# Ten weight blocks and the first chunk's output in transfers of 120 and 8 partitions

## The reference

```python
def one_chunk(xc):                       # 128 tokens
    q = (xc @ w_q).reshape(PEER_CHUNK, PEER_HEADS, 2, PEER_HALF)
    sc = jnp.einsum('chid,hikd->chik', q, sub_keys)
    top_s, top_i = lax.top_k(sc, PEER_TOPK)
    ...
    expert = i1 * PEER_KEYS + i2
    gate = jax.nn.softmax(best_s, axis=-1)
    u_e = jnp.take(u_tab, expert, axis=0)
    v_e = jnp.take(v_tab, expert, axis=0)
    act = jax.nn.gelu(jnp.einsum('chkd,cd->chk', u_e, xc))
    return jnp.einsum('chk,chkd->cd', gate * act, v_e)

for l in range(DEPTH):
    h = rmsnorm(x, norm_mix_g[l])
    proj = h @ w_in[l]
    ...
    x = x + y @ w_out[l]
    x = x + memory_cross_attention(rmsnorm(x, norm_mem_g[l]), rmsnorm(mem, mem_norm_g[l]),
                                   w_mq[l], w_mkv[l], w_mo[l])
    x = x + peer_ffn(rmsnorm(x, norm_ffn_g[l]), peer_wq[l], peer_sub_keys[l], peer_u[l], peer_v[l])
return rmsnorm(x, final_norm_g)
```

## Time and profile before

| | |
|---|---|
| median of 3 runs | 1695.9 us (1695.7 to 1696.14) |
| the profiled execution's span | 1694.8 us |
| median less span | 1.1 us |
| PE busy | 1540.1 us (91%) |
| DVE busy | 1176.0 us (69%) |
| ACT busy | 734.3 us (43%) |
| POOL busy | 578.1 us (34%) |
| moved by DMA | 675.13 MB, mean 398 GB/s |
| of it by the gathers' queue | 536.90 MB |
| of it by SP's queue | 136.74 MB |

### The profile page before, as it was taken

How to read it: one execution, slowest core, us unless ns; L and a number is a source line. 1 busy time by engine, 2 the same in 40 slices (tenths; PEclk the granted TensorE clock), 3 DMA queues, 4 the chain that set the end, 5 groups by cost and what they waited for, 6 DMA issues and landing times.

```text
span 1694.8 us, 19255 instructions
## 1 busy us (share of the span) xinstructions
PE 1540.1 (91%) x6354; PEld 893.8 (53%) x6354; DVE 1176.0 (69%) x2993; ACT 734.3 (43%) x1963; POOL 578.1 (34%) x527
## 2 busy tenths in 40 slices
PE   9999999889999999988989889988999998777786
PEld 8757775347567656434645446434756554222232
DVE  7821899975877658987555667995556676666655
ACT  4142534763464333484433353465444334333333
POOL 0000444442334334443333433342333444343331
PEclk9999999999999999999999999999999999999999
DMA  9655999999999999999999999999999999999996
GB/s 384 257 199 223 376 422 421 421 421 420 420 420 421 420 419 421 413 422 422 420 421 421 416 421 421 392 417 391 421 413 413 421 421 422 422 421 421 421 421 276
DMA packets 94003, 675.13 MB, mean 398 GB/s; under 512 B 10424, under 2 KB 10704, under 8 KB 12496
## 3 DMA queue, kind: packets, MB, share of 16 engines
q0 software_dynamic: 73728, 536.90, 76.5%
q1 hardware_dynamic: 20032, 136.74, 19.9%
q10 hardware_dynamic: 144, 0.26, 0.0%
HBM read 672.81 MB, written 1.05 MB: 398 GB/s over the span
## 4 chain that ended last, share of the span: by engine, by line
PE 35%; DMA 35%; DVE 9%; ACT 4%; issue 2%; POOL 0%; DVEq 0%; ACTq 0%; POOLq 0%
DMA slots<-expert_rows,expert 35%; PE bank L1007 19%; PE bank L477 7%; DVE slots L2027 5%; PE bank L680 3%; PE bank L974 2%; PE bank L990 2%; ACT diag L1518 1%; ACT coef L1536 1%; DVE sg L1563 1%; DVE htok L1850 1%; PE bank L767 1%; ACT gel L1531 0%; DVE x L1563 0%; ACT L1531 0%
## 5 line engine op out<-in xcount | busy, mean ns | idle before, releaser
L1007 PE MATMUL bank<-slots,diag 128*128 128x512 f32 x1914 | 902.6, 607 | 129.3 <-ACT diag L1518 123.0
L1142 POOL DMA_INDIRECT slots<-expert_rows,expert x512 | 576.2, 1125 | 1092.7 <-PE bank L1007 876.7
L2027 DVE CUSTOM_DVE_ANT_0 slots<-slots,htok 128x1024 f32<-128x1024 f32 x512 | 625.7, 1223 | 389.5 <-DMA slots<-expert_rows,expert 388.5
L1007 PEld LDWEIGHTS bank<-slots,diag 128*128 128x128 f32 x1914 | 346.3, 192 | 546.3 <-issue 324.3
L1531 ACT ACTIVATE gel<-dot 128x2 f32<-128x2 f32 (+1 forms) x258 | 52.5, 203 | 652.2 <-DVE dot L2027 651.5
L477 PEld LDWEIGHTS bank<-hT,ring 128*128 128x128 f32 x1488 | 180.1, 192 | 42.1 <-issue 40.6
L477 PE MATMUL bank<-hT,ring 128*128 128x128 f32 x1488 | 181.2, 276 | 1.5 <-ACT hT L1178 1.0
L1518 ACT ACTIVATE diag<-ident,coef 128x128 f32<-128x128 f32 x479 | 168.2, 394 | 8.6
L1536 ACT ACTIVATE coef<-gel,gexp 128x1 f32<-128x1 f32 x512 | 123.1, 287 | 10.4
L1531 ACT ACT_TABLE_LOAD x67 | 86.0, 1283 | 1.2
L1563 DVE SCALAR_TENSOR_TENSOR sg<-pad,prm,sg 128x128 f32<-128x128 f32 x240 | 71.5, 342 | 0.0
(11 more groups left out here) (359 smaller groups left out, 1475.2 us busy)
## 6 DMA issues: line engine op xcount, KB each, us to landing
ring<-w_blocks SPq DMA_DIRECT2D x89, 1024.0 KB, 9.3
slots<-w_blocks SPq DMA_DIRECT2D x24, 1024.0 KB, 11.1
slots<-expert_rows,expert POOLq DMA_INDIRECT x512, 16.0
kept<-w_blocks SPq DMA_DIRECT2D x4, 1024.0 KB, 12.6
keys<-w_blocks SPq DMA_DIRECT2D x2, 1024.0 KB, 10.4
kv<-w_blocks SPq DMA_DIRECT2D x2, 1024.0 KB, 14.0
prm<-small SPq DMA_DIRECT2D x2, 768.0 KB, 12.7
x<-x_rows SPq DMA_DIRECT2D x2, 512.0 KB, 11.4
```

The lines of the kernel that those rows point to most:

```text
L1007: last = mm(bank[h][:, :], diag[:, i % DIAGS, :], slots[:, SLOT[n], D + h * 512:D + (h + 1) * 512], start=m == 0, stop=n == end - (ph == N ...
L1142: nc.gpsimd.indirect_dma_start(slots[:, s, :], None, (experts0_d, experts1_d)[n // PER // NC], bass.IndirectOffsetOnAxis(ap=idx[q % 2][:, ...
L2027: v.tensor_tensor_reduce(out=slots[:, s, 0:D], in0=slots[:, s, 0:D], in1=htok[:, ph % 2, :], scale=1.0, scalar=0.0, op0=ALU.mult, op1=ALU.add,
```

## The change

`PARTED` names, for stage 1, 2 and 3, three, three and four blocks: `out` 18, `mq` 23 and `mo` 27 in stages 1 and 3, `wq` 31 in stage 3 as well, and `q` 4, `mv` 14 and `mo` 25 in stage 2. Each goes in two transfers, partitions 0 to 119 (`MOST` = 120) and 120 to 127. Both add 16 to `loaded` of the place, so PE waits for the sum of parts (`in_by`). The two stores of the first chunk are split in the same way; `stored` then counts six transfers, four of chunk 0 and two of chunk 1.

```diff
+PARTED = {1: (18, 23, 27), 2: (4, 14, 25), 3: (18, 23, 27, 31)}
+MOST = 120
...
+        def parts(j):
+
+            l, n = order[j]
+            return 2 if n in PARTED.get(NC * l + second[j], ()) else 1
+
+        def in_by(j):
+
+            p, n = spots[j]
+            return 16 * sum(parts(i) for i in range(j + 1) if spots[i][0] == p)
...
-                    eng.wait_ge(loaded[p], 16 * (spots[j][1] + 1))
+                    eng.wait_ge(loaded[p], in_by(j))
...
-                nc.sync.dma_start(home(p), blocks_d[l * NBLK + n, :, :]).then_inc(loaded[p], 16)
+                if parts(j) == 2:
+                    nc.sync.dma_start(home(p)[0:MOST, :], blocks_d[l * NBLK + n, 0:MOST, :]).then_inc(loaded[p], 16)
+                    nc.sync.dma_start(home(p)[MOST:P, :], blocks_d[l * NBLK + n, MOST:P, :]).then_inc(loaded[p], 16)
+                else:
+                    nc.sync.dma_start(home(p), blocks_d[l * NBLK + n, :, :]).then_inc(loaded[p], 16)
...
-                    nc.sync.dma_start(out_d[c * P:(c + 1) * P, i * 512:(i + 1) * 512],
-                                      outs[c][:, i * 512:(i + 1) * 512]).then_inc(stored, 16)
-            eng.wait_ge(stored, 16 * 2 * NC)
+                    for a, b in ((0, MOST), (MOST, P)) if c == 0 else ((0, P),):
+                        nc.sync.dma_start(out_d[c * P + a:c * P + b, i * 512:(i + 1) * 512],
+                                          outs[c][a:b, i * 512:(i + 1) * 512]).then_inc(stored, 16)
+            eng.wait_ge(stored, 16 * (4 + 2))
```

## The result

The changed kernel takes 1744.1 us in the median of four runs (1743.8 to 1745.7), against 1696.0 us before: a ratio of 1.0284, 95% interval 1.0271 to 1.0296. It is 48 us slower, 44 us over my forecast and 30 us over the end of my range. The mechanism was among the rivals, but its price was not.

A forecast was written before the change was run, and what follows sets the result against it. The DMA engines, through the one that ends last, were taken to bound the kernel. Span 1694.8 + 3.5 (blocks) + 0.2 (output) = 1698.5 us; with 1.1 us from span to median, 1699.6 us. Range 1689 to 1714 us.

The forecast's parts named there:

- The bound and the straggler: DMA engines set the pace; the slowest ends some 5.0 us behind the second, with a 9.2 us tail after it.
- Which engine it is: The engine that ends last was taken as one of the eight that get one row more per changed block.
- term (1): Ten split blocks: each gives the last engine one more row plus a packet and completion, 0.35 us; 3.5 us in all.
- The shares of engines: 120 rows go to 15 engines, 8 each, and 8 rows to 8 engines, one each; one engine may get none.
- SP's issues and PE's waits for 32: SP's 12 further issues, 4 us in all, and PE's waits for 32 increments on split blocks cost nothing.
- a sign against this term: PE waiting for `ring` more than a few us in total would show the free SP issues wrong.
- The output: First chunk's output, two transfers become four: two more 2 KB rows and two more completions, 0.2 us.
- the price of a row off the whole block's pattern: Off-pattern 8 KB rows in changed blocks were priced after the `gains` transfers, which cost only 0.04 and 0.08 us.
- The upper bound: Most the changed blocks could cost: each row meets another engine's in SBUF and takes twice as long, 28 us.
- The rival: Rows of split blocks, dealt off their engines' own partitions, collide beside gathers: 14 us more, 1713.6 us; chance 0.24.
- half of nine rows: The collision rival's sizing: half of the nine rows in each changed block take twice as long, 14 us.
- the forecast case: One more row per changed block for the last engine, without collisions: 1698.5 to 1701 us; chance 0.42.

The follow-up runs named there:

- The spread rows: Kernel before plus 28 HBM-to-HBM transfers of eight, seven or fifteen 8 KB rows, every second row of a larger array: 1704.85, 1704.88 and 1705.33 us, against 1696.81.
- fifteen and eight singly: Kernel before, but of the ten blocks only the 120-partition transfers are issued, or only the 8-partition ones: 1731.92 us and 1684.49 us.
- the column halves: Kernel before with the ten blocks each in two transfers of 128 partitions by half the columns, output whole: 1696.95 us, ratio 1.0004.
- the fifteen spread rows: Kernel before plus 28 HBM-to-HBM transfers of fifteen 8 KB rows each, every second row of a larger array: 1705.33 us, ratio 1.0051.

## Why the prediction was wrong

**The bound and the straggler: right.** DMA sets the pace, one engine ends last, alone for some 5 us, and 9.2 us follow its last landing; all of that stands unchanged in the trace after.

**Which engine it is: right.** I took it to be one of the eight from 0.04 and 0.08 us in the earlier trace rows, thin evidence, so there was luck in it. The spread rows confirm it, if transfers to HBM and to SBUF use the same engines. With their 0.29 us a row (forecast: 0.35 with its packet and completion), term (1) comes to 2.9 us where I had 3.5. In the changed kernel itself no run isolates that term.

**The shares of engines: right.** 84 completions more, and fifteen and eight singly.

**SP's issues and PE's waits for 32: right.** Nothing, by the column halves. PE's waits for `ring`, 5.0 us, were more than the few us that I had named as a sign against this term. They follow from the collisions, not from the issues: the column halves have the same issues and wait 1.1 us, and in PE's longest wait the DMA engines stay busy at a low rate:

```profile
401.90:405.30 3.40, 0.01 (x1) 0.04 (x1) 0.00 (x0) 0.00 (x0) 0.94 (x1) 0.87 0.98 265
```

**The output: 0.2 us forecast, about 1 us measured.** That is a difference of two medians whose ranges meet, and no more than a hint. It is the same kind of transfer, with rows of 2 KB.

**The step that failed: the price of a row off the whole block's pattern.** The prediction said: "No row shows off-pattern transfers of 8 KB; the nearest, the `gains` ones, cost only 0.04 and 0.08 us, and I follow them." That row was near in kind and far in size. A `gains` transfer is eight packets under 2 KB on eight engines, one each; the part of 120 partitions alone is 120 rows of 8 KB, and the block is in flight for some ten microseconds. Its cost was not that of an extra row on one engine but of everything that was in flight beside it.

**The upper bound was wrong too,** and this is the more instructive step. "Every row of a changed block meets another engine's row at the same place in SBUF and takes twice as long. That is nine rows of 0.310 us more in ten blocks, 28 us." When two rows meet, both are slow, and the other one is often a gather's. While a changed block lands, an engine moves its eight or nine rows of the block and at least as many of gathers: in ten microseconds at 0.55 us a row, 18 rows. Each takes 0.24 us more than 0.31: 4.3 us a block, 43 us in ten. With the extra row of 2.9 us and the output's 1.1 us that is an estimate of 47 us, against the 48 measured. The queues' shares give the same size without it: 29 us in gathers' rows and 18 us in SP's. The numbers for it stood in my own text: rows of both queues at 0.310 us, a block that lands 9.3 us after its issue, engines without any idle time. Counting whatever is in flight for those 9.3 us, about thirty rows an engine at the old pace, would have given a bound above the result. The range did not even hold the bound that I had: 28 us over the median is 1724 us, and the range ended at 1714.

**The rival was the right one, mis-sized.** "Rows off their engines' own partitions collide" had 24% and 1713.6 us. Its mechanism is the one that the trace shows, down to the sign it named, a rate well under 420 GB/s at a full DMA share. Its "half of nine rows" should have been nearly all rows of both queues. And the forecast case is not another case beside it: by the shares the straggler had its extra row while the collisions happened. I had put as alternatives what could add up.

**What the mechanism rests on.** Shown: column halves cost nothing (1.0004), partition halves with the same engines and shares 39 us, and a split block with no gathers beside it already moves at 0.58 us a row. Not shown: which engine read which row and wrote to which partition, since no view has it; so that the rows meet in SBUF, and not in HBM, is argued, with the fifteen spread rows for it. The Trainium skill, page "DMA: Bandwidth & Descriptors", section "The descriptor swizzle", says that in a transfer of 128 partitions each engine writes to the eight partitions of one SBUF port, its own; transfers of other counts are not covered by that formula. The trace agrees as far as it goes: with every engine on its own port nothing would meet, in blocks and gathers alike, and rows take 0.31 us. By the map of the Trainium skill, page "SBUF — State Buffer", section "Door 1: The DMA port swizzle", partitions 0 to 63 reach eight of sixteen ports, which would halve the rate, and the 221 GB/s of one window against 414 fits. But by the same map 120 partitions reach all sixteen, and the rate fell to 209 to 246 between 264 and 272 us all the same. So the number of ports reached is not what decides here; that two engines go to the same port at the same time would fit the runs, without giving the sizes, and that last step is argued, not measured. I had drawn on that second page in the prediction for the eight partitions only, the part that turned out to be cheap (1 us a block), and not asked what it meant for the 120.

## What to carry to other kernels

Split a transfer by columns, not by partitions, when another stream keeps the DMA engines busy: halves of columns were free here, halves of partitions cost 3.9 us for each MB. The Trainium skill, page "DMA: Bandwidth & Descriptors", section "Rules for kernel authors", says of two transfers to disjoint partition halves not to bother since they serialize; here they did worse, they slowed the other stream.

When a change can make packets slower, price every packet that is in flight at the time, of all queues, not those of the changed transfer; and look for the loss in the rate under a full busy row, since a busy DMA row hides it.

Rivals that can happen together belong in one sum. Here the extra row, some 3 us, and the collisions, the remaining 44 us of the blocks' 46.8, were such a pair; the division between them is an estimate.

## What the runs showed of the hardware

- A row of 8 KB takes 0.31 to 0.32 us in blocks of 128 partitions. In blocks cut in 120 + 8 or 64 + 64 it takes 0.54 us beside gathers, whose rows then take 0.56 us too; in 112 + 16 it is 0.48 and 0.49 us. With no gathers beside it, 120 + 8 takes 0.58 us a row.
- 120 partitions go to 15 engines and 8 to 8, by the count of completions (10 and 80 fewer than with whole blocks), and 112, 64 and 16 to all sixteen (160 more in ten split blocks).
- Eight rows that lie together in HBM, copied to HBM, are cut in sixteen pieces, and seven too; rows with gaps between them stay whole, on as many engines as there are rows (8, 7 and 15).
- The engine that ends last is one of the seven that carry such a transfer of seven rows. The Trainium skill, page "DMA: Bandwidth & Descriptors", section "Latency and other measured facts", calls engines 7 and 15 usually slower; by the numbering of that page's section "Why a DMA increments its semaphore by 16 and not by 1", lowest first, the seven would be 0 to 6, so this straggler would be neither. No view here numbers engines, and what makes it late stays open.
- It also stays open why rows are slowed less in 112 + 16 partitions (3.2 us a block) than in 120 + 8 (4.7 us). No kernel of this study was faster than the kernel before and computed the same; the column halves equal it.
